# Scan preparation two product tiles earlier, and a store wait moved ahead of a phase barrier, in one step of a hybrid attention / RWKV-7 layer

## The reference

```
proj = modulate(rmsnorm(x)) @ w_in        # columns: q, k, v | u (RWKV input) | ga, gr (two gates)
u    = dwconv3(u) -> r, k, v, wd, ad, gd  # r, k, v 512 wide; wd, ad 64; gd 128
kk   = (k * k_k) * rsqrt(sum_per_head((k * k_k)**2) + 1e-12)
for each direction:
    w = exp(-exp(-softplus(-(w0 + tanh(wd) @ w2)) - 0.5));  a = sigmoid(a0 + ad @ a2)
    y = scan over tokens of the state update with r, w, k * (1 + (a-1)*ka), v, kk, a
rwkv   = groupnorm(y0 + y1) ... * (sigmoid(gd) @ g2)
merged = sigmoid(ga) * (attention @ w_attn) + sigmoid(gr) * (rwkv @ w_rwkv)
x = x + gate1 * (merged @ w_out);  x = x + gate2 * gated_mlp(modulate(rmsnorm(x)))
```

## Time and profile before

| what | value |
|---|---|
| median of 3 runs | 1461.8 us (1459.86 to 1461.96) |
| the profiled execution | 1459.86 us, of which 1458.1 us is the span of the trace |
| PE busy | 1327.9 us, 91% of the span |
| DVE / ACT / POOL busy | 50% / 36% / 3% |

### The profile page before, as it was taken

One profiled execution on the slowest core, in us unless ns is written; L12 is line 12 of the kernel. 1 busy time (PEld: TensorE's weight loads), 2 busy tenths in 40 slices (PEclk: granted clock), 3 DMA queues, 4 the chain that ended last, 5 costly groups with the idle time before them and its releaser, 6 DMA issues.

```text
span 1458.1 us, 31772 instructions
## 1 busy us (share of the span) xinstructions
PE 1327.9 (91%) x13955; PEld 1222.8 (84%) x13955; DVE 730.3 (50%) x1085; ACT 530.0 (36%) x796; POOL 41.8 (3%) x84
## 2 busy tenths in 40 slices
PE   4799999997998799869993989989999999989996
PEld 2799999997997555569973968889999999989995
DVE  3517742734554389955544532165454545433534
ACT  3635534422334343313342211264343433333333
POOL 0000010000000000000001000000000000000000
PEclk9899999999999799989996999999999999999998
DMA  9222264313000200020006477211212211022222
GB/s 395 79 97 94 103 264 166 104 46 161 8 4 3 87 0 1 1 96 8 4 3 242 148 279 271 89 59 58 86 62 82 78 66 65 15 59 77 66 74 93
DMA packets 24761, 134.58 MB, mean 92 GB/s; under 512 B 2992, under 2 KB 3632, under 8 KB 16208
## 3 DMA queue, kind: packets, MB, share of 16 engines
q1 hardware_dynamic: 19088, 103.59, 19.9%
q0 software_dynamic: 5568, 29.40, 5.4%
HBM read 112.66 MB, written 20.32 MB: 91 GB/s over the span
## 4 chain that ended last, share of the span: by engine, by line
PE 83%; DVE 8%; ACT 3%; DMA 3%; issue 2%; PEld 1%; POOLq 0%; PEldq 0%; POOL 0%; SPq 0%; DVEq 0%; ACTq 0%
PE ps L675 45%; PE ps L1120 11%; PE ps L838 4%; PE ps L826 3%; PE ps L806 2%; PE ps L1025 2%; PE ps L710 1%; PE ps L984 1%; PE ps L818 1%; DMA xT<-in_x 1%; DVE rden L1802 1%; PE ps L700 1%; PE ps L1002 1%; DMA bld<-branch_scratch 1%; PE ps L949 1%
## 5 line engine op out<-in xcount | busy, mean ns | idle before, releaser
L675 PE MATMUL ps<-h2lo,whi 128*128 128x322 f32 x672 | 154.5, 311 | 0.7 <-ACT facc L1220 0.7
L675 PE MATMUL ps<-h2hi,wlo 128*128 128x322 f32 x672 | 155.0, 312 | 0.0
L675 PE MATMUL ps<-h2hi,whi 128*128 128x322 f32 x672 | 154.0, 310 | 0.0
L1512 DVE TENSOR_TENSOR wlo<-raw,whi 128x2048 fp32r<-128x2048 f32 x48 | 109.7, 2287 | 72.4 <-ACT whi L1182 72.4
L675 PE MATMUL ps<-hlo,whi 128*128 128x322 f32 x544 | 127.8, 316 | 1.0 <-ACT qkv L1246 1.0
L675 PE MATMUL ps<-hhi,wlo 128*128 128x322 f32 x544 | 125.4, 312 | 0.0
L675 PE MATMUL ps<-hhi,whi 128*128 128x322 f32 x544 | 124.7, 310 | 0.0
L675 PEld LDWEIGHTS ps<-h2hi,whi 128*128 128x128 f32 x672 | 114.2, 190 | 0.0
L675 PEld LDWEIGHTS ps<-h2lo,whi 128*128 128x128 f32 x672 | 113.0, 189 | 0.9 <-DVE wlo L1512 0.9
L675 PEld LDWEIGHTS ps<-h2hi,wlo 128*128 128x128 f32 x672 | 113.6, 189 | 0.0
L1556 DVE SCALAR_TENSOR_TENSOR facc<-fraw,par,facc 128x642 f32<-128x642 f32 x44 | 39.1, 888 | 139.2 <-ACT facc L1220 139.2
(11 more groups left out here) (312 smaller groups left out, 2636.9 us busy)
## 6 DMA issues: line engine op xcount, KB each, us to landing
raw<-in_wblk SPq DMA_DIRECT2D x48, 1024.0 KB, 4.9
adl<-in_wada SPq DMA_DIRECT2D x8, 2048.0 KB, 8.2
raw<-in_wdn SPq DMA_DIRECT2D x44, 256.0 KB, 2.6
adaw<-in_wada SPq DMA_DIRECT2D x4, 2048.0 KB, 17.5
gate_scratch<-gout POOLq DMA_DIRECT2D x16, 322.0 KB, 2.5
gld<-gate_scratch POOLq DMA_DIRECT2D x8, 644.0 KB, 4.1
attention_inputs_used<-attention_scratch SPq DMA_DIRECT2D x1, 5056.0 KB, 14.6
u_scratch<-uout POOLq DMA_DIRECT2D x12, 320.0 KB, 2.4
```

Of the source, the lines that this page charges most:

```text
L675: mm = pe.matmul(o, w, v, start=first, stop=last and w is hi and x is xh[n])
L1512: TT(wlo[s][:, :], raw[s][:, :], whi[s][:, :].bitcast(F32), ALU.subtract).then_inc(lo_done, 1)
```

## The change

Steps of the preparation stand behind an earlier gate tile on all three engines: the key squares behind t = 0 instead of 2, their products and norms behind t = 1 instead of 3, and the four rounds e behind t = 2 to 9 instead of 4 to 11. POOL's wait for the last gate stores is moved from behind its first constant copies (`presets(0)`) to ahead of the second barrier.

```
@@ gpsimd
                 gp.dma_start(gate_s[i, :, s, :], gout[s][:, :]).then_inc(g_st[s], 16)
+        for s in range(2):
+            gp.wait_ge(g_st[s], 16 * NBLK_G)
         phase_over(gp, 2)
@@
         presets(0)
-        for s in range(2):
-            gp.wait_ge(g_st[s], 16 * NBLK_G)
         phase_over(gp, 3)
@@ tensor, between_gates(t)
-            if t == 3:
+            if t == 1:
                 for s in range(2):
                     prepare_product(0, s)
-            elif t % 2 == 0 and 4 <= t < 12:
+            elif t % 2 == 0 and 2 <= t < 10:
                 for j in range(2):
-                    prepare_product(0, t - 2 + j)
+                    prepare_product(0, t + j)
@@ scalar
                 if t == 0:
                     low_tanh()
-                elif t == 2:
                     key_squares(0)
-                elif t == 3:
+                elif t == 1:
                     ...
-                elif 4 <= t < 12 and t % 2 == 0:
+                elif t < 10 and t % 2 == 0:
                     ...
@@ vector
-            if 4 <= t < 12:
-                for part in range((3 if t % 4 == 2 else 4) if t % 2 == 0 else 2):
+            if 2 <= t < 10:
+                for part in range((4 if t % 4 == 2 else 3) if t % 2 == 0 else 2):
                     next(first)
```

More of the change, by code:

```diff
@@ L1328, in _ @@
                         key_norm(0, s)
-                elif 4 <= t < 12 and t % 2 == 0:
+                elif t < 10 and t % 2 == 0:
                     for n in range(2):
[L1331 to L1334, removed]
+                        prep_tanh(0, t // 2 - 1, n)
+                    key_factor(0, t // 2 - 1)
+                elif t < 10:
+                    prep_decays(0, t // 2 - 1)
         phase_over(ac, 2)
```

## The result

The changed kernel takes 1471.93 us (median of 4 runs, 1469.04 to 1472.65), beside 1460.89 us of the kernel before on the same chip: 11.0 us slower, ratio 1.0074 with a 95% interval of 1.0058 to 1.0089. The forecast was slower, by 5.85 us; the time lies 0.6 us beyond the upper end of the range. The profiled execution took 1468.41 us with a span of 1466.6 us, 8.5 us over that of before.

What follows compares the result with a forecast made beforehand. PE bounds the kernel (83% of the chain), and nothing waits for the preparation. Stall 5.9, clock 1.3 and barrier -1.35 sum to +5.85 us, on a median of 1461.8 giving 1467.6 us; range 1463.6 to 1471.3.

Steps and rivals of the forecast that it cites:

- Part 1: Behind gate tile 1: PE waits for the key squares, whose loads land late; gate tile 2 delayed, costing 5.9 us.
- the rival of a sooner landing: Second uc load lands at 223.7 us, stall costs only 2.65 us, total 1463.1 us; chance 9%.
- a landing by about 219 us: Bound for the second uc load, 0.7 us after its issue, at which the stall would be gone.
- Part 2: Behind the stall: granted clock falls to 0.50 for about 3 us, costing 1.3 us; bounds nothing and 2.5 us.
- Part 3: Second barrier: POOL waits for the last store's landing, then drains 0.14 us; barrier opens sooner, -1.35 us.
- the -1.35 of the sum: Second barrier's term in us: opening at about 332.8 instead of 334.16 us.
- The prediction's own sign of this: Forecast is wrong if PE's tile 15 to the first scan product takes longer than 5.2 us.
- The bound of +2.5: Second barrier: POOL's drain takes its full 4.2 us from the landing at 332.5 us, costing 2.5 us.
- a fixed time after the issue: Second barrier: drain ends 4.2 us after the last store's issue at 329.96 us, so the barrier term is 0.
- the barrier grows: Second barrier: drain takes its full length after the landing; 9.7 us slower in total, 1471.5 us; chance 8%.

Runs made afterwards that it cites:

- e9: Changed kernel, with POOL loading the k third of both uc first, each with its own semaphore; 1462.65 us, ratio 1.0016 to the kernel before.
- e7: Changed kernel with 32 unused matmuls added on PE inside its stall behind gate tile 1; 1468.27 us, ratio 1.0051 to the kernel before.
- e4: Changed kernel with one more POOL drain, ahead of its wait for the last gate tile; 1468.1 us, ratio 1.0051 to the kernel before.
- e8: Changed kernel with one more POOL drain, ahead of gate tile 8; no run time given, drain at the second barrier 0.71 us for 8 DMAs.
- e14: Changed kernel with one more POOL drain, ahead of the hpw and uc loads; no run time given, second barrier's drain 1.69 us for 20 DMAs.
- e2: Kernel before with only POOL's wait for the gate stores moved ahead of the second barrier; 1462.39 us, ratio 1.0008 to the kernel before.
- e12: Kernel before, unchanged, traced a second time; no run time given, gate stretch 115.28 us.
- e5: Kernel before with one more POOL drain, ahead of its wait for the last gate tile; 1458.15 us, ratio 0.9990 to the kernel before.
- e6: Kernel before with POOL signing the second barrier by an empty instruction instead of a drain; 1454.04 us, ratio 0.9961 to the kernel before.
- e13: Changed kernel, unchanged, timed again; 1472.05 us against 1460.98 us, ratio 1.0065 to the kernel before.

## Why the prediction came out too low: the step that failed, and the rest

**Part 1, the stall, held.** 5.9 us were forecast, as idle stretches of some 2 and some 3.5 us; they are 2.60 and 2.45. In the changed trace gate tile 2 starts at 231.29 instead of 220.8 + 1.7 (this trace's later start) = 222.5; less 2.16 us of products and less 1.4 us by which the second product is slower, it is 5.3. The second `uc` took 8.0 us to land, as before about 8.6: a load issued ahead of the gate stores isn't hurried by their absence, and the rival of a sooner landing falls (5.4 would have been needed). One reading in it is too strict: the stall was said to be gone only with a landing by about 219 us. If the first square starts by 220.0, the second ends in time when it starts by 221.1, since PE has the first product to do meanwhile; e9, with squares at 219.6 and 220.8 when the start of its trace is set to that of before, lost 0.2 us.

**Part 2, the clock, was mis-sized.** I had 3 us of work at the lower level; it was 4.2, from 228.8 to about 233, and I had priced it with dense matmuls, 1.3 us. The second product fell into it too: 2.47 us with its tail instead of 1.08, so 1.4, and tile 2 took 8.01 instead of 7.15, so 0.9. Together 2.25 us, and e7 has 2.1 by a direct comparison. Parts 1 and 2 give 7.5 where 7.2 were forecast; that it comes so near is luck in part, since the two errors nearly cancel.

**Part 3, the barrier, failed.** The step was that the drain takes 0.14 us when it begins after the landing, as at the fourth barrier. It took 3.33 us, so the -1.35 of the sum was really +1.7, an error of 3.1 us and of the sign. The prediction's own sign of this came up: from the end of PE's tile 15 to the first scan product it is 6.97 us, where more than 5.2 was to mean that it is wrong. Besides, the first scan products ran 0.5 us longer at the lower clock (4.36 against 3.86 us), a term that the sum didn't have. I had taken the row with the same order of instructions, but the drain's length goes by the number of DMAs since the last drain (e4, e8, e14): 1 there, 40 here. The bound of +2.5, the full old drain behind the landing, held it. The old 4.17 us weren't a fixed time after the issue either, the other reading that I gave: they were the issue of the last store (0.54 us) and the settling of 40 DMAs behind it (3.34 by the line), with 0.3 us over that stay open. The rival "the barrier grows", given 8%, is the case that happened; its 1471.5 us is within 0.5 us of the time measured. The nearness is luck: it stands for +9.7 us on a median of 1461.8, and measured were +11.0 on 1460.9, and it took the drain as 4.2 us instead of 3.3.

**The rest.** 7.5 to 8.0, 1.7 and 0.5 make 10 us, beside 9.5 and 10.8 by the ratios and 11 by the medians; up to 1 us stays open. Two things in the table bear on it. The way to the first tanh took 213.7 to 216.4 us; the two traces of the changed kernel lie 1.7 us behind the two of before there, but e4, with both edits, at 214.15 and e2, with one, at 215.87, so I don't call it an effect. It isn't ruled out either: the four traces that keep the old order and the old wait (before, e12, e5, e6) are all at 213.7 to 214.3, and the twelve others go from 213.7 to 216.4. And in the scan, some 14 us behind the barrier, PE stands idle for 0.8 to 2 us, and in some executions the clock falls once more behind that (before: 39.24 us to `out_ns`, e13: 39.72), in others not (changed: 38.01). What decides it was not tried. The range erred by putting only 8% on the one bound of Part 3 that had no row against it but that of another barrier.

## What to carry to other kernels

Work moved ahead to a place where nothing waits for it can only lose: its gain is zero from the start, and its price is whatever its inputs are late by, paid by the engine whose list it blocks, and what the lower clock adds behind the idle time. Ask of each moved step when its last input lands, by the trace, and how much room the new place leaves; here 7.15 us decided everything. And a drain of GpSimd took time in proportion to the DMAs before it: keep it out of a barrier that the other engines wait at, by a drain where GpSimd idles or by signing without one where only DMAs precede.

## What the runs showed of the hardware

- GpSimd's drain took 0.055 us and 0.082 us for each DMA that it had issued since its last drain, though all had landed, most of them long ago (1 to 42 DMAs: e4, e8, e14, the changed kernel, e9), and 20 DMAs took 1.70 us with 9.5 MB and 1.69 with 7.6 (e14). Begun with the issue of a store it took 0.8 to 1.2 us more (before, e4, e5, e8), and with one DMA just issued it lasted 2.57 us, about until that had landed (e5).
- At the lower clock behind the stall a pair of fp32 matmuls of 512 columns took twice its time: 2.04 us in the changed kernel against 1.02 for the same two matmuls in e7. The clock fell at about 226.7 us there, with PE idle but for one pair of short products since 222.5 us (0.56 in the window from 226 to 228), and came back at 233.1.
- Fillers of no use between waits kept the granted clock at 1.00 through the stall, which was worth 2.1 us from the second product on (e7).
